# Expert lists from a DRAM table, and a tail with the second gate and early sums on TensorE

## The reference, cut to what matters

```python
scores = sigmoid(t @ router_w)                      # 384 x 64
idx = group-limited top 8 of scores + router_bias
w = scores[idx] / sum(scores[idx]) * 2.5
hid = silu(t @ exp_w_gate[e]) * (t @ exp_w_up[e])   # 64 experts, 1024 -> 256
routed = sum over the token's 8 experts of w * (hid @ exp_w_down[e])
ff = routed + shared(t)
x = x + gate2 * ff
y = rmsnorm(x, final_g)
```

## Time and profile before

| | |
|---|---|
| median of 3 runs | 1185.79 us (1184.06 to 1187.43) |
| profiled execution, its own time | 1187.37 us |
| its span | 1185.6 us |
| PE, DVE, ACT, POOL busy | 95%, 87%, 67%, 20% of the span |
| mean DMA rate | 278 GB/s |
| share of the chain that ended last | PE 75%, DVE 9%, DMA 8%, ACT 5% |

### The profile page before, as it was taken

How to read it: one execution, slowest core, us unless ns; L and a number is a source line. 1 busy time by engine, 2 the same in 40 slices (tenths; PEclk the granted TensorE clock), 3 DMA queues, 4 the chain that set the end, 5 groups by cost and what they waited for, 6 DMA issues and landing times.

```text
span 1185.6 us, 16767 instructions
## 1 busy us (share of the span) xinstructions
PE 1125.1 (95%) x5625; PEld 918.9 (78%) x5625; DVE 1034.8 (87%) x1382; ACT 796.4 (67%) x992; POOL 235.0 (20%) x182
## 2 busy tenths in 40 slices
PE   4999999998999999989999999999999999999984
PEld 1799999864557798658888888888888888888851
DVE  4769999989996565869998999999999999999977
ACT  6543232767873632748887888888888888888831
POOL 1000000001123001223422323332323323222210
PEclk8999999998999989999999999999999999999997
DMA  9673446635547227859999999999999999999994
GB/s 349 183 182 107 143 148 171 182 116 173 163 122 235 80 78 274 326 216 343 378 362 356 365 373 369 377 363 346 354 354 365 359 358 380 364 374 365 357 416 178
DMA packets 123259, 329.10 MB, mean 278 GB/s; under 512 B 28248, under 2 KB 69815, under 8 KB 98375
## 3 DMA queue, kind: packets, MB, share of 16 engines
q1 hardware_dynamic: 98656, 290.39, 66.8%
q0 software_dynamic: 21584, 33.79, 8.4%
q10 hardware_dynamic: 2968, 4.26, 1.0%
HBM read 327.70 MB, written 41.66 MB: 312 GB/s over the span
## 4 chain that ended last, share of the span: by engine, by line
PE 75%; DVE 9%; DMA 8%; ACT 5%; issue 2%; SPq 0%; POOL 0%; DVEq 0%; ACTq 0%; POOLq 0%
PE bank L1746 19%; PE bank L1748 19%; PE bank L1747 19%; PE bank L1756 7%; DMA raw<-in_exp_w_down_dram 3%; DVE lgu L1455 2%; DMA y_d<-ys,ixt 2%; PE bank L1941 2%; ACT hi L816 2%; PE bank L1929 1%; DVE lo L1584 1%; PE bank L1762 1%; DMA row1b<-y_d 1%; DMA raw<-in_mod_w_dram 1%; PE bank L1763 1%
## 5 line engine op out<-in xcount | busy, mean ns | idle before, releaser
L1455 DVE TENSOR_TENSOR lgu<-raw,hgu 128x2048 fp32r<-128x2048 f32 x128 | 292.0, 2282 | 1.3 <-ACT hgu L1069 1.3
L1069 ACT ACTIVATE hgu<-raw 128x2048 fp32r<-128x2048 f32 x128 | 245.4, 1917 | 0.4 <-DMA raw<-in_exp_w_gate_dram 0.4
L1746 PE MATMUL bank<-hgu,xgh 128*128 128x512 f32 x512 | 205.8, 402 | 2.4 <-DVE lgu L1455 2.1
L1748 PE MATMUL bank<-hgu,xgl 128*128 128x512 f32 x512 | 200.6, 392 | 0.0
L1747 PE MATMUL bank<-lgu,xgh 128*128 128x512 f32 x512 | 199.2, 389 | 0.0
L1584 DVE TENSOR_TENSOR lo<-raw,hi 128x2048 fp32r<-128x2048 f32 x64 | 147.7, 2308 | 27.8 <-ACT hi L1078 20.1
L1186 DVE TENSOR_TENSOR lo<-raw,hi 128x2048 fp32r<-128x2048 f32 (+2 forms) x57 | 125.8, 2209 | 29.9 <-ACT hi L816 29.9
L776 POOL DMA_INDIRECT xg<-h_d,ixt x64 | 66.3, 1036 | 399.1 <-DVE gsl L1557 372.5
L1078 ACT ACTIVATE hi<-raw 128x2048 fp32r<-128x2048 f32 x64 | 122.9, 1921 | 28.4 <-DMA raw<-in_exp_w_down_dram 28.4
L1284 DVE SCALAR_TENSOR_TENSOR zb<-zb,cwt 128x400 f32<-128x400 f32 x240 | 135.7, 634 | 0.6
L785 POOL DMA_INDIRECT y_d<-ys,ixt x62 | 124.7, 2011 | 48.3 <-ACT ys L1111 28.6
(11 more groups left out here) (306 smaller groups left out, 2081.0 us busy)
## 6 DMA issues: line engine op xcount, KB each, us to landing
raw<-in_exp_w_gate_dram SPq DMA_DIRECT2D x64, 1024.0 KB
raw<-in_exp_w_up_dram SPq DMA_DIRECT2D x64, 1024.0 KB
raw<-in_exp_w_down_dram SPq DMA_DIRECT2D x64, 1024.0 KB
raw<-in_mod_w_dram SPq DMA_DIRECT2D x20, 1024.0 KB, 5.2
raw<-in_w_in_dram SPq DMA_DIRECT2D x16, 512.0 KB, 5.4
raw<-in_w_in_dram SPq DMA_DIRECT2D x8, 1024.0 KB, 5.4
mraw<-in_mod_w_dram SPq DMA_DIRECT2D x4, 1024.0 KB, 15.7
raw<-in_w_o_attn_dram SPq DMA_DIRECT2D x4, 1024.0 KB, 5.0
```

Of the source, the lines that this page charges most:

```text
L1069: act.activation(hgu[k % 2][:, :, w, :], src, ACT.Copy).then_inc(ghi_done, 1)
L1455: dve.tensor_tensor(lgu[k % 2][:, :, w, :], src, hgu[k % 2][:, :, w, :].bitcast(F32), ALU.subtract).then_inc(glo_done, 1)
L1746: pe.matmul(out, ah, bh, start=first, stop=False)
L1748: return pe.matmul(out, al, bh, start=False, stop=last)
```

## The change

The first three quarters of the diff move the lists. After the routing, VectorE works out for every token its eight entries (token, destination, gate) and the row of a DRAM table `lists_d` where each belongs (`entry_rows`, before the loop, and `entry_gates`, in step 0). GpSimd fills the table at the start of the kernel (a constant that is out of bounds as an index), writes the 24 x 128 entries with indirect DMAs in steps 0 to 6, and loads the table back to SBUF as `listed` in step 7. Experts 0 to 10 still get their lists as before; from 11 (`ON_TENSOR`) on, `token_list` and `onehot` are gone, and `list_of` is two copies out of `listed`, placed at the end of VectorE's step.

In the tail, the two broadcasts of the gate row give way to two loads of the row alone on GpSimd's queue; TensorE spreads each over 128 partitions with a matmul by ones and ScalarE copies that to `tg`. For tiles 1 and 2 TensorE adds `acc` (rows 0 to 4) into its PSUM sum, so VectorE multiplies the whole sum once and adds x1. Several semaphores are merged under one name.

```diff
+TAIL_SUMS = 4 * NT + 4
+KEY = 2048
+ON_TENSOR = UNROLL + 3
...
+    parts["key"] = np.broadcast_to(KEY * (NE - np.arange(NE))[None, :], (P, NE))
+    parts["dest"] = (TOPK * parts["token"][:, :, None] + np.arange(TOPK)).reshape(P, NT * TOPK)
...
             sp.wait_ge(dn_filled, N2)
-            for cc in range(2):
-                sp.dma_start(tg[:, cc, :], mod_row(5, cc).partition_broadcast(P)).then_inc(tail_in, 16)
             sp.wait_ge(x1_out, 48)
...
             pool.memset(zb[:, :, :], 0.0).then_inc(zeros_done, 1)
+            pool.wait_ge(con_in, 16)
+            pool.dma_start(lists_d.rearrange("(q a) v -> q (a v)", q=P).rearrange("q (b n) -> q b n", n=P),
+                           ones.unsqueeze(1).to_broadcast([P, NJ * 4 // P, P])).then_inc(lists_out, 16)
...
+            def write_lists(first, end):
+
+                if first == 0:
+                    pool.wait_ge(lists_out, 16)
+                    pool.wait_ge(entry_done, 1)
+                for n in range(first, end):
+                    t, u = n // TOPK, n % TOPK
+                    pool.indirect_dma_start(lists_d, bass.IndirectOffsetOnAxis(ap=entry_row[:, t, u:u + 1], axis=0),
+                                            entry[:, t, u, :], None,
+                                            bounds_check=P * NJ - 1, oob_is_err=False).then_inc(lists_out, 16)
+
             def step(i, k, left=99):
                 j = i * UNROLL + k
                 if left > 3:
                     gather(i, k + 3)
                 if from_step(j, 3):
                     scatter(i, k - 3, last=left <= -1)
+                if isinstance(j, int) and j < 7:
+                    write_lists(24 * j // 7, 24 * (j + 1) // 7)
+                if isinstance(j, int) and j == 7:
+                    pool.wait_ge(lists_out, 16 * (NT * TOPK + 1))
+                    pool.dma_start(listed[:, :, :], lists_d.rearrange("(q j) v -> q j v", q=P)).then_inc(lists_out, 16)
...
             in_order(pool, step)
+            for cc in range(2):
+                pool.dma_start(g2s[:, cc, :], mod_row(5, cc)).then_inc(g2s_in, 16)
...
             act.activation(stat[:, 63:64], stat[:, 48:49], ACT.Sqrt)
+            for cc in range(2):
+                act.wait_ge(g2_filled, cc + 1)
+                for b in range(2):
+                    ins = act.activation(tg[:, cc, 512 * b:512 * b + 512], psum[6 + b][:, :], ACT.Copy)
+                ins.then_inc(g2_done, 1)
...
                 if from_step(j, UNROLL):
                     dve.wait_ge(scattered[k % 2], uses(i, k - UNROLL) * 16)
+                if not isinstance(j, int) or j >= ON_TENSOR:
+                    dve.wait_ge(lists_out, 16 * (NT * TOPK + 2))
+                    dve.tensor_copy(ixt[:, k % UNROLL, :], listed[:, bass.ds(j, 1), 0:2].rearrange("p a v -> p (a v)").bitcast(I32))
+                    dve.tensor_copy(gsl[:, k % UNROLL:k % UNROLL + 1],
+                                    listed[:, bass.ds(j, 1), 2:3].rearrange("p a v -> p (a v)")).then_inc(list_done, 1)
+                    return
...
+            def entry_gates():
+
+                for t in range(NT):
+                    for u in range(TOPK):
+                        ins = dve.scalar_tensor_tensor(out=key_gate[:, u, :], in0=keys[:, t, :], scalar=key8[:, t, u:u + 1],
+                                                       in1=rgate[:, t, :], op0=ALU.is_equal, op1=ALU.mult,
+                                                       accum_out=entry[:, t, u, 2:3])
+                    if t < NT - 1:
+                        link(dve, "v", ins)
+                ins.then_inc(entry_done, 1)
+                dve.wait_ge(entry_done, 1)
...
-                if left > 3:
+                if isinstance(j, int) and j + 3 < ON_TENSOR:
                     list_of(i, k + 3)
-                if left > 4:
+                if isinstance(j, int) and j + 4 < ON_TENSOR:
                     onehot(i, k + 4)
                 if left > 1:
                     turn_lo(i, k + 1)
+                if isinstance(j, int) and j == 0:
+                    entry_gates()
...
+                if left > 3 and not (isinstance(j, int) and j + 3 < ON_TENSOR):
+                    list_of(i, k + 3)
...
             shared_hidden(2)
+            entry_rows()
             in_order(dve, step)
...
-                dve.wait_ge(tail_in, 96)
+                dve.wait_ge(tail_in, 64)
+                dve.wait_ge(g2_done, 2)
...
             def finished(t):
 
+                base = acc[:, 0, :] if t == 0 else tx[:, t, :]
...
-            based(1)
-            based(2)
+            plus_shared(0)
             plus(5, 0)
-            plus_shared(0)
...
-                if left > 3:
+                if isinstance(j, int) and j + 3 < ON_TENSOR:
                     token_list(i, k + 3)
...
+            def spread(cc):
+
+                for b in range(2):
+                    ins = pe.matmul(psum[6 + b][:, :], ones[0:1, :], g2s[:, cc, 512 * b:512 * b + 512], start=True, stop=True)
+                ins.then_inc(g2_filled, 1)
+
+            def early_sum(t):
+
+                pe.wait_ge(sum_done, 3 * NT + t + 1)
+                for b in range(2):
+                    pe.matmul(psum[shared_banks[t][b]][:, :], ident, acc[:, t, 512 * b:512 * b + 512],
+                              start=False, stop=False)
+
+            last_out = value(pe, last * UNROLL + UNROLL)
+            pe.wait_ge(rtab_done, 1)
+            pe.wait_ge(ys_done, last_out)
+            pe.wait_ge(g2s_in, 32)
+            spread(0)
+            early_sum(1)
+            early_sum(2)
+            pe.wait_ge(g2_done, 1)
+            spread(1)
             for n in (5, 6, 7):
```

More of the change, by code:

```diff
@@ L276, in hybrid_step @@
         gsl = sb("gsl", [P, UNROLL], R + 8.375)
+        listed = sb("listed", [P, NJ, 4], R)
+        entry = sb("entry", [P, NT, TOPK, 4], A + 7.25)
+        entry_row = sb("entry_row", [P, NT, TOPK], A + 7.625, I32)
+        keys = sb("keys", [P, NT, NE], R + 14)
+        key_gate = sb("key_gate", [P, 8, NE], R + 12)
+        key8 = sb("key8", [P, NT, TOPK], R + 15)
+        key_i, key_p, key_q, key_r = (sb(f"key_{n}", [P, NT, TOPK], R + 15.125 + 0.125 * i, I32)
+                                      for i, n in enumerate("ipqr"))
         sg = sb("sg", [P, FF], R + 9)
@@ L289, in hybrid_step @@
         tg = sb("tg", [P, 2, D], A + 57)
+        g2s = sb("g2s", [1, 2, D], R)
         fgr = sb("fgr", [P, D], A + 105)
@@ L299, in hybrid_step @@
         y_d = dram("y_d", [T * TOPK, D])
+        lists_d = dram("lists_d", [P * NJ, 4])
         def conv_slot(k):
@@ L341, in hybrid_step @@
         cks_out = sem("cks_out")
[L342 to L343 removed]
+        zeros_done, sig_done, z_done, conv_step = (sem(n) for n in ("zeros_done", "sig_done", "z_done", "conv_step"))
+        sgs_out = [sem(f"sgs_out{i}") for i in range(2)]
         qtok_done, qrope_done, qT_act, qT_dve = (sem(n) for n in ("qtok_done", "qrope_done", "qT_act", "qT_dve"))
@@ L1550, in list_of @@
                     p = got(dve, ("list", j))
-                else:
+                elif isinstance(j, int) and j < ON_TENSOR:
                     dve.wait_ge(list_filled, j - 1)
@@ L1601, in hidden, with entry_rows @@
                                          op0=ALU.mult, op1=ALU.mult).then_inc(hd_done, 1)
+            def entry_rows():
+                first = pos3[:, :, 0:NE]
+                link(dve, "v", dve.scalar_tensor_tensor(out=keys[:, :, :], in0=first, scalar=512.0,
+                                                        in1=key_of.unsqueeze(1).to_broadcast([P, NT, NE]),
+                                                        op0=ALU.is_lt, op1=ALU.mult))
+                link(dve, "v", dve.tensor_tensor(keys[:, :, :], keys[:, :, :], first, ALU.add))
+                for t in range(NT):
+                    ins = dve.max(key8[:, t, :], keys[:, t, :])
+                dve.tensor_copy(entry[:, :, :, 0].bitcast(I32), token.unsqueeze(2).to_broadcast([P, NT, TOPK]))
+                for v in (1, 3):
+                    dve.tensor_copy(entry[:, :, :, v].bitcast(I32), dest)
+                link(dve, "v", ins)
+                link(dve, "v", dve.tensor_copy(key_i[:, :, :], key8[:, :, :]))
+                dve.tensor_scalar(key_p[:, :, :], key_i[:, :, :], 7, 4, ALU.bitwise_and, ALU.logical_shift_left)
+                dve.tensor_scalar(key_r[:, :, :], key_i[:, :, :], 1, NE * 3, ALU.logical_shift_right, ALU.bitwise_and)
+                link(dve, "v", dve.tensor_scalar(key_q[:, :, :], key_i[:, :, :], 3, 15, ALU.logical_shift_right, ALU.bitwise_and))
+                link(dve, "v", dve.tensor_tensor(key_p[:, :, :], key_p[:, :, :], key_q[:, :, :], ALU.add))
+                dve.tensor_scalar(key_q[:, :, :], key_i[:, :, :], 11, None, ALU.logical_shift_right)
+                link(dve, "v", dve.scalar_tensor_tensor(out=key_p[:, :, :], in0=key_p[:, :, :], scalar=float(NJ),
+                                                        in1=key_r[:, :, :], op0=ALU.mult, op1=ALU.add))
```

(2 more changed lines are left out.)

48 lines of the change are left out of this document (26 added, 22 removed).

## The result

The changed kernel takes 1283.38 us (median of 4 runs, 1277.23 to 1289.12), the kernel before beside it 1184.94: a ratio of 1.083, with an interval of 1.080 to 1.085. I had forecast 1243 and a range of 1180 to 1292. The sign was right, the value 40 us too low, and the time lies close to the rival "gather blocked" (1280), though, as it turned out, not for that rival's reason.

The account below looks back on a forecast made before the run. TensorE, VectorE (96%) and DMA (95%) were taken as near-equal bounds. 1187.4 + 49 (loop) + 2 (VectorE) + 9 (writes) + 0.5 (filling) - 3 (tail) = 1244.9, less 1.6 for the profiled run: 1243 us, range 1180 to 1292.

Parts of the forecast that it names:

- gather blocked: Rival: in its new place the gather stands 2 us for lgu; +86 in place of +49, 1280 us; chance 0.22.
- the late list closes a loop: VectorE's late list delays gather and scatter; rows_out two steps on waits for the scatter: two steps at least 10.80 + S.
- the gather's own loop: Second loop in the expert steps: 9.49 plus the gather's landing, plus some 1 us of transposes, less 1.10.
- the loop term: Expert loop: a step of 10.6 us, 0.93 more than now, over 53 steps: +49 us.
- S: Issue to landing of the scatter in the loop: taken as 10.4 us, between 7.9 and 15.3.
- Scatter in time: Rival: with S of 8.0 or less TensorE stays the bound of the loop; 1173 us; chance 0.15.
- the rule of the Trainium skill: GpSimd-issued transfers: 2.0 us plus bytes over 436 GB/s, about 2.5 us per scatter; nothing would stall.
- The saving on TensorE: List matmuls gone for 53 experts: 0.23 us per step, 12 us if TensorE stayed the bound.
- Writes and VectorE: Before and early in the loop: list writes +9 us, entry_rows and entry_gates +2, table filling and constants +0.5.
- List writes clog GpSimd: Rival: each list write takes 5.1 us in steps 0 to 6; +72 in place of +9, 1306 us; chance 0.08.
- The table's load: Loading the finished table, 0.39 MB behind step 7's scatter, has a step and a half: costs nothing.
- Tail: After the loop: without two 512 KB broadcasts late rows arrive 2.6 us sooner, VectorE does less; -3 us (0 to -5).

Follow-up runs that it names:

- e2: Kernel before with list_of(k+3) at the end of VectorE's step from step 8 on, lists still from TensorE: 1250.4 us, ratio 1.055.
- e3: Changed kernel with GpSimd's scatter(k-3) ahead of its gather(k+3) in each step: 1245.6 us, ratio 1.049.
- e11: Kernel before with one constant changed, so its lists hold positions on the table's SBUF partitions: 1214.5 us, ratio 1.024.
- e10: Changed kernel with the list in its old early place and the table addressed in the partition order of the kernel before: 1198.6 us, ratio 1.010.
- e1: Changed kernel with list_of(k+3) back in its old place ahead of turn_lo, lists still from the table: 1232.4 us, ratio 1.040.
- e12: Changed kernel with a one-input VectorE op in place of lgu's first half (gate weights) from expert 9 on: 1280.5 us, ratio 1.080.
- e14: Changed kernel with lgu's first half in four pieces of 128x512 from expert 9 on, same values: 1283.7 us, ratio 1.082.
- e5: Changed kernel with a VectorE memset of 128x400 ahead of gate_up_lo(k+1, 0) from step 9 on: 1282.2 us, ratio 1.082.
- e6: Kernel with the new tail, the table written but never loaded or read, lists from TensorE: 1203.6 us, ratio 1.017 to the kernel before.
- e4: Kernel before with only the new tail (gate rows spread by TensorE, early sums on TensorE), no table: 1182.2 us, ratio 0.998.

## Why the prediction was right or wrong

**That the late list closes a loop, and where: right.** The gather came at 9.35 behind ys for 9.49, ys waits for y_d, TensorE is idle, and e2 shows that the place alone does it. e3 shows the gather's own loop right behind it, at 10.5.

**The step that failed is the size of the loop term:** "(10.80 + 10.4)/2 = 10.6 us, 0.93 more than now, over 53 steps: +49 us". It measured 11.17 and +76. Two things were in it that I had not put there. First, the order of the rows: I read the diff's key arithmetic as the same list in another place, and costed a changed partition for each token at nothing. It costs 0.42 per step where the kernel is otherwise the one before (e11) and 0.55 with the early list (e10 against e1). Between e2 and the changed kernel, which differ in the source of the lists and the work for them as well, the step differs by 0.26; how much of that is the order was not tried. Second, I built the loop as the scatter's start plus a landing S of its own. Measured in e2, where the order is the old one, start and landing are 12.4 and 9.3: both ends wrong, their sum 21.8 and not 21.2. What stayed the same from run to run is one number, about 12.4 us from the gather's start (13.0 with the table's order) to the ys two steps on. The kernel before has its pair elsewhere in the step, so its trace does not hold this number; e2 gives it. I took S from one scatter and never asked what it would be with another distance to the gather, which lay 1.3 us ahead of it. That my 10.4 lies near the landings of 9.3 (e2) and 10.2 (changed kernel) is in part luck: it is 15.30 less 3.8 for a long span on GpSimd and about 1 for idler DMA. The 1.01 in that difference is the gather's span in rows 6, where the scatter's own was 3.08, and in e12 and e14 a shorter span of the pair on GpSimd brought no landing forward.

**The rival that came closest, "gather blocked", had the right row and the wrong price.** The span did go from 1.01 to 2.98 in 44 of 53 gathers; but e12 and e14 shortened it, to 1.92 and 1.38, the scatter started 0.7 us sooner in the mean (11.5 for 12.2), and no time came back. That no block at all would cost nothing either was not tried. The traces give a hint: in eight steps of the changed kernel the gather spans 1.02 (the scatter then 2.0 to 2.6) and the scatter starts 10.70 behind ys; there ys two steps on comes 12.9 us behind the gather's start, against 13.1 in 41 steps with the long span. In e5 seven such steps have 12.1 against 13.1. **"Scatter in time"** fell: it needs a landing of 8.5 or less, and e2 has 9.3 even behind a scatter that starts 1.6 us later than I had it. So did the rule of the Trainium skill behind it (DMA: Bandwidth & Descriptors, anatomy of a SWDGE DMA, about 2.5 us for such a transfer): the landings measured here are more than three times as long. That what is ahead in the queue and on the engines makes the difference is likely, not shown.

**The saving on TensorE (0.23 per step, 12 us) was real but hidden;** in e10 the mean step is 9.47 for 9.71, and the loop from step 10 to 62 takes 12.8 us less.

**Writes and VectorE: +9, +2 and +0.5 predicted.** e6 is 12.0 us behind e4 at step 10: right. "List writes clog GpSimd" fell, though it was near: GpSimd is busy almost without a break from 533 to 612 us, a third of the write spans about 1.0, most others 1.9 to 2.9, two above 4.5, as in

```profile
567.95 2.05 POOL L816 DMA_INDIRECT lists_d<-entry,entry_row  x1 [0.30 <-issue]
570.31 1.90 POOL L816 DMA_INDIRECT lists_d<-entry,entry_row  x1 [0.30 <-issue]
572.51 0.97 POOL L816 DMA_INDIRECT lists_d<-entry,entry_row  x1 [0.30 <-issue]
```

**The table's load, costed at nothing, was wrong.** It is issued at 615.35 in the changed kernel, when the last write has landed, not behind step 7's scatter (611.71), and VectorE waits for it, even in the late place:

```profile
DVE ixt L1600 <- DMA listed<-lists_d: 3.9, 1, 3.9
```

In e10, whose list is early, that wait is 13.1. Together the head of the loop cost 19.8 us (4.6 + 15.2) for the 11.5 that I had.

**Tail: -3 predicted, -2.8 in e4, for another reason, so by luck.** I had put the gain on rows that land 2.6 us sooner. The late sums start only 0.7 us nearer to the last ys; the other 2.0 are TensorE's clock (e4 above), which I had in no term: work in the gap keeps it at its upper level. Whether the spreads or the early sums do it was not tried apart. In the changed kernel the late sums take 8.79 as well, but start 26.2 us behind the last ys, and only 0.5 of the gain shows. Of the 2.2 us against e4, 1.6 are eight matmuls at half clock on the way out of the loop, as the chain shows behind a wait:

```profile
1235.35 0.24 PE bank L1836
1235.59 0.43 PE bank L1837
1236.01 0.43 PE bank L1838
1236.44 0.43 PE bank L1836
```

## What to carry to other kernels

When the place of an instruction feeds a transfer through another engine's queue, count the loop from the first transfer of the pair to the release of the buffer as well as from the second, and don't take a landing measured at one spacing of the two as a constant at another. When indices are permuted, ask on which partitions the real rows come to lie, even if the set is the same: here 0.4 us of a 9.7 us step hung on one constant. A table that is written row by row must be costed to its last landing and the load behind it, not to its issues; in e10 the head of the loop lost 25.6 us by the table, and the faster loop gave 12.8 back. Work put into a gap of TensorE can be worth more than the work itself, by the clock of what follows: here 2.0 us of a tail.

## What the runs showed of the hardware

- The order of 48 real rows over 128 partitions moved the mean DMA share from 0.95 to 0.91 and the rate from 362 to 347 GB/s, with loads always waiting (e11 against the earlier trace rows).
- A one-input op of VectorE (128x2048, 1.22 us, so twice the pace of the two-input one) stretches a gather on GpSimd from 1.0 to 1.92 us (e12). The Trainium skill (SBUF — State Buffer, section on who interferes with whom) names both kinds, an op with two SBUF inputs and `tensor_scalar` in its faster mode with two ports, and the traces agree; its inference that an op with two inputs would not hold up the making of descriptors does not fit the 2.98 us of the gathers here.
- TensorE's granted clock fell to 0.97 in the loop, once waits of 1 to 4 us came into it (1.00 before). In the rows above a matmul goes from 0.24 to 0.43 us, from the level of 2.4 GHz to that of 1.2 GHz, 1.4 us after TensorE had come back from an idle stretch of 2.33 us. Eight matmuls of 128x512 took 5.63 us behind a wait of 8.05 us and 3.70 behind work without a gap (before and e4).
- A scatter of some 48 rows of 4 KB lands 9.2 us (e2), 10.5 (e3), 10.8 (e1) or 10.9 (e14) behind its start, as medians beside the stream of weight loads, and a gather 8.7 to 11.0 in the same runs.
